# Two chained blocks on one core: up slabs on the input without its norm factor, embedding in rounded products, gate halves and residual rows in other banks

## The chip, the cores and the metric

One core of one Trainium2 chip runs the whole program. The metric is the device time of one execution in microseconds (us). The trace is that of one profiled execution; its span runs from its first to its last instruction.

## What is computed

256 tokens of width 1024 go through two blocks, one after the other, in float32. The first block has two attentions and an output projection, then a gated feed-forward layer with a short convolution over time, then a gated embedding:

```
x = x + rms_norm(mix, g_post_mix)
h = rms_norm(x, g_pre_ffn)
u = causal_depthwise_conv(h @ w_up, conv_w, conv_b)      # 1024 -> 2 x 2816, three taps
gate, val = split(u)
x = x + rms_norm((gelu(gate) * val) @ w_down, g_post_ffn)
e = p @ w_ple                                            # 256 -> 1024
g = sigmoid(rms_norm(x, g_ple_gate) @ w_ple_gate + b)
x = x + rms_norm(g * e, g_post_ple)
```

The second block modulates its norms by a condition (`mod = silu(c) @ mod_w + mod_b`), has a convolution, a sparse attention and a pooling mixer, and ends in a mixture of 32 experts (1024 -> 512 -> 1024, two experts for each token, their residual added), whose 96 weight slots of 2 MB each are all read. A last rms_norm gives the output.

## The kernel before

Each engine has a program of its own, written out by hand: `tensor` (PE), `scalar` (ACT), `vector` (DVE), `gpsimd` (POOL) and `sync` (SP). They meet only in semaphores: `wait_ge(name[key])` waits for the instruction that was issued with `then_inc(name, key)`. Each engine works strictly in its written order, so a wait holds everything behind it. SP issues all DMAs in the order of the list `STREAM`, into a ring of seven slots of 2 MB; before each it waits until the slot's last content was used (`BEFORE`, `used`). One late `used` holds all loads behind it.

A weight product is made of three "rounded" products. ACT writes the rounded weight (`hi`), DVE or POOL the rest (`lo` = weight - `hi`), the input has the same two parts, and PE multiplies `hi*hi`, `hi*lo` and `lo*hi`. There are four places for weight pairs (`weight_place`), so ACT can round at most four tiles ahead of PE. `POOL_UP` lists the rests that POOL makes. Other products are plain float32 and take PE two instructions each.

The stages that matter here, in order:

- **Output projection (`wo`)**, and after it `to_features("mix")`: PE turns the tokens back to features, DVE adds them to the residual `xT` in eight steps (`add_turned`). ACT squares `xT` (`x_squares`), PE sums the squares over features (`token_sums`), ACT copies, PE makes columns (`token_columns`), ACT takes the root and DVE its reciprocal (`joint_row`), and PE spreads the factor over all partitions (`turned_over`).
- **Up, 11 slabs (`wup`)**: only then does DVE multiply `xT` by gain and factor into `yT` (`h`), ACT round it, DVE make its rest, tile by tile. A slab j is 8 tiles k, each with 4 column blocks x 3 products of 128x256, that is 96 products in two PSUM banks. While slab j runs, `conv_step(j-1, step)` makes convolution, gelu and product of slab j-1: ACT the base tap, DVE two more taps for each of the two banks, ACT gelu, POOL the product and a rest.
- **Down (`wdown`)**: 44 weight tiles, in each 6 products of 128x512. DVE also makes 16 sums (`mod_column`) for the second block, each with a weight slot (`modw`) that SP can replace only when its fourth sum is made.
- **Embedding and gate**: `embed` has four products groups of two float32 products, in banks 5 and 6, between the turns of the tokens; `gate` has three rounded products per tile, with its halves in the banks `ZB`.
- **Second block**, up to `route`: PE adds `wout2`, DVE adds to `xT`, ACT squares, POOL and DVE add the squares, PE sums them (`cols`). `token_major` turns `xT` into rows by four times four transposes (banks `TOKB`), ACT scales them (`h`), and `over_tokens` brings the same rows into the banks `YB` once more, by products with the identity, in which the experts' sums are then accumulated: two of the four before the routing's products, two behind the first eight expert slots of group 0.
- **Experts**: 8 groups of 12 slots. After the first slots, slots 12, 13 and 14 are loaded in halves of 1 MB, each into the half of the ring that a used slot of group 0 left.

## Time and profile before

| | us |
|---|---|
| median of 3 runs | 919.2 (918.31 to 919.8) |
| profiled execution, its own time | 917.52 |
| its span | 915.6 |
| PE busy / DVE busy / ACT busy / POOL busy in the span | 769.0 / 383.0 / 328.8 / 128.0 |
| data read and written | 298.48 MB |

Busy shares are means over stages of different kinds. The chain of waits (the work that ended last, followed back) tells which engine or transfer set the end at each time, and the table of stretches what the others did meanwhile.

### The profile page before, as it was taken

To read this page: it belongs to the slowest core of one execution; us is meant where nothing else is said; L and a number is where in the kernel's file an instruction comes from. 1 tells how busy PE (TensorE), PEld (TensorE's weight loads), DVE (VectorE), ACT (ScalarE), POOL (GpSimd) and SP (SyncE) were. 2 spreads that over 40 slices of the span, in tenths; PEclk is the share of its full clock that TensorE was granted. 3 is DMA by queue.
4 is the path that set the end of the run, shared out by engine and by line. 5 is a ranking of instruction groups with operands and counts; after the bars stand their busy time and mean duration, and the time that the engine had idled before them with its cause. 6 is when DMAs were issued, how large, how long until landed. Compare 5 with 4: busy or idle time off the path is not lost.

```text
span 915.6 us, 12692 instructions
## 1 busy us (share of the span) xinstructions
PE 769.0 (84%) x5298; PEld 527.4 (58%) x5298; DVE 383.0 (42%) x838; ACT 328.8 (36%) x656; POOL 128.0 (14%) x130
## 2 busy tenths in 40 slices
PE   9999999999999999999999985668675575655575
PEld 7986579999998867898785431223221222212223
DVE  5757776667779764899613110010100100101002
ACT  5756767666665467824723010001000000000012
POOL 0021042555541033103010000000000000000000
PEclk9999999999999999999999997878778887887877
DMA  9956709755069782646579999999999999999995
GB/s 356 422 193 230 318 1 374 292 185 184 2 278 394 280 337 78 263 175 229 220 306 356 428 447 420 431 434 432 437 433 422 432 437 425 436 432 428 432 421 241
DMA packets 19359, 298.48 MB, mean 326 GB/s; under 512 B 2144, under 2 KB 2528, under 8 KB 5856
## 3 DMA queue, kind: packets, MB, share of 16 engines
q1 hardware_dynamic: 19296, 297.61, 78.7%
q8 instruction: 43, 0.70, 0.3%
q14 instruction: 20, 0.16, 0.1%
HBM read 296.55 MB, written 1.05 MB: 325 GB/s over the span
## 4 chain that ended last, share of the span: by engine, by line
PE 56%; DMA 30%; DVE 9%; ACT 3%; issue 1%; SPq 0%; DVEq 0%; ACTq 0%
PE ps L114 56%; DMA ring<-in_exps 30%; DVE ar L140 3%; DVE fr L132 2%; ACT L120 1%; DVE ar L132 1%; DVE hT L140 0%; ACT sq L120 0%; PE ps L117 0%; ACT ar L123 0%; DVE xg L140 0%; ACT ar L120 0%; ACT yT L120 0%; DVE yT L140 0%; ACT hT L120 0%
## 5 line engine op out<-in xcount | busy, mean ns | idle before, releaser
L114 PE MATMUL ps<-fr 128*128 128x256 f32 (+2 forms) x1308 | 206.7, 314 | 1.1 <-ACT fr L120 0.4
L114 PEld LDWEIGHTS ps<-fr 128*128 128x128 f32 (+1 forms) x1308 | 182.9, 189 | 19.3 <-issue 2.1
L114 PE MATMUL ps<-ring,sq 128*32 128x512 f32 x944 | 129.7, 703 | 74.9 <-DMA ring<-in_exps 74.5
L114 PE MATMUL ps<-ring,ar 128*32 128x512 f32 (+4 forms) x792 | 97.1, 594 | 49.4 <-DMA ring<-in_exps 45.4
L114 PEld LDWEIGHTS ps<-ring,sq 128*32 128x32 f32 x944 | 31.8, 126 | 163.6 <-DMA ring<-in_exps 87.9
L132 DVE TENSOR_TENSOR fr<-ring,fr 128x512 fp32r<-128x512 f32 (+1 forms) x120 | 93.8, 808 | 40.2 <-ACT fr L123 40.1
L132 DVE TENSOR_TENSOR ar<-ar,ps 128x512 f32<-128x512 f32 x9 | 6.2, 687 | 242.3 <-PE ps L114 241.3
L114 PEld LDWEIGHTS ps<-ring,ar 128*32 128x32 f32 (+1 forms) x792 | 29.8, 125 | 101.5 <-issue 50.9
L123 ACT ACTIVATE fr<-ring 128x512 fp32r<-128x512 f32 (+1 forms) x139 | 80.1, 622 | 22.6 <-PE ps L114 20.0
L123 ACT ACTIVATE ar<-ps 128x512 f32<-128x512 f32 (+4 forms) x48 | 27.2, 571 | 153.6 <-PE ps L117 130.7
L132 DVE TENSOR_TENSOR ar<-ps,ar 128x512 f32<-128x512 f32 (+6 forms) x38 | 23.4, 632 | 120.5 <-PE ps L114 120.2
L114 PE MATMUL ps<-ar 128*128 128x512 f32 (+10 forms) x328 | 65.6, 418 | 8.0 <-DVE ar L132 6.9
L120 ACT ACTIVATE sq<-ps,misc 128x128 f32<-128x128 f32 x31 | 11.9, 456 | 166.3 <-PE ps L114 166.3
L114 PE MATMUL ps<-fr,fr_h 128*128 128x256 f32 x552 | 69.7, 282 | 0.0
L114 PEld LDWEIGHTS ps<-fr,fr_h 128*128 128x128 f32 x552 | 67.7, 191 | 0.0
L114 PEld LDWEIGHTS ps<-ar 128*128 128x128 f32 (+4 forms) x328 | 36.8, 172 | 39.1 <-issue 18.8
L132 POOL TENSOR_TENSOR ar<-ar 128x128 f32<-128x128 f32 (+2 forms) x21 | 11.2, 533 | 312.5 <-DVE ar L132 311.4
L123 ACT ACTIVATE fr_h<-ring 128x512 fp32r<-128x512 f32 x66 | 40.2, 630 | 17.7 <-PE ps L114 17.6
L120 ACT ACTIVATE ar<-ps 128x768 f32<-128x768 f32 (+1 forms) x21 | 14.8, 715 | 83.3 <-PE ps L114 81.9
L114 PEld LDWEIGHTS ps<-ar,yT 128*128 128x128 f32 x256 | 30.4, 192 | 11.8 <-issue 11.5
L140 DVE SCALAR_TENSOR_TENSOR yT<-ps,cols,yT 128x255 f32<-128x255 f32 (+1 forms) x88 | 37.2, 472 | 0.0
L132 DVE TENSOR_TENSOR fr_h<-ring,fr_h 128x512 fp32r<-128x512 f32 x43 | 31.3, 730 | 13.6 <-ACT fr_h L123 13.5
(193 smaller groups left out, 896.5 us busy)
## 6 DMA issues: line engine op xcount, KB each, us to landing
ring<-in_exps SPq DMA_DIRECT2D x21, 4096.0 KB, 28.4
ring<-in_exps SPq DMA_DIRECT2D x10, 6144.0 KB, 26.9
ring<-in_modw SPq DMA_DIRECT2D x12, 2048.0 KB, 13.8
ring<-in_exps SPq DMA_DIRECT2D x12, 2048.0 KB, 12.6
ring<-in_wup SPq DMA_DIRECT2D x11, 2048.0 KB, 14.0
ring<-in_wdown SPq DMA_DIRECT2D x5, 2048.0 KB, 12.7
ring<-in_exps SPq DMA_DIRECT2D x9, 1024.0 KB, 10.8
ring<-in_win SPq DMA_DIRECT2D x4, 2048.0 KB, 11.2
```

What stands on the lines that cost most here:

```text
L114: return Issue(self.e and self.e.matmul(o, l, r, start=start, stop=stop, skip_group_check=True))
L120: return Issue(self.e and self.e.activation(o, i, f, **kw))
L123: return Issue(self.e and self.e.activation(o, i, ACT.Copy, scale=scale))
L132: return Issue(self.e and self.e.tensor_tensor(o, a, b, op))
L140: return Issue(self.e and self.e.scalar_tensor_tensor(out=o, in0=a, scalar=s, in1=b, op0=op0, op1=op1))
```

## The change

It has seven parts.

1. **Up input without the factor.** `x_hi` is now the rounded `xT * g_pre_ffn`, its rest `x_lo` follows from `xT` directly; the factor's row is made while PE works on slabs 0 and 1 and is multiplied into each slab's two result banks (`normed`, 22 DVE instructions in place in PSUM) before the convolution.
2. **Orders around it.** ACT, DVE and POOL have another order in slabs 0 and 1 and in `conv_step` (steps 3, 4, 5, 8, 9); squares are added in pairs by POOL, so that PE has four column sums in place of eight; PE makes them behind slab 0, the columns behind tile (1,0), the row behind tile (1,1). The banks of the slabs are swapped (`FB`). `mod_column` in slabs 7 to 10 stands at k = 7 in place of k = 1.
3. **Second modulation third earlier.** `mod_sum(1)` and `mod_total(1)` move from the stretch before slab 0 into the output projection.
4. **`crow`** has a place of its own and is loaded earlier, its silu moves to slab 4.
5. **Embedding** in three rounded products each; ACT and POOL make the parts of `p` and `w_ple` in the down stage.
6. **Gate halves** in other banks (`ZB`), so that the first half no longer waits for the last embedding copy; in the second block's start half a `modw` slot is worked off in quarters (`mod_quarter`).
7. **Route.** `token_major` brings the rows once, by products, straight into `YB`, where ACT reads them; `over_tokens` goes. Squares are summed by PE in two steps without DVE's addition. The halves of slots 12 to 14 take other places: half 0 of slot 12 goes to `xT`, as soon as the rows are turned, each other half one place earlier.

```
-POOL_UP = {("lo", 0, k) for k in (0, 1, 2, 3, 5, 7)} | ...
+POOL_UP = {("lo", 0, k) for k in range(6)} | ...
-        FB = (0, 1, 4, 5)
+        FB = (4, 5, 0, 1)
-        ZB = {(0, 0): 6, (1, 0): 7, (0, 1): 0, (1, 1): 1}
+        ZB = {(0, 0): 0, (1, 0): 7, (0, 1): 6, (1, 1): 1}
+        def half_place(j, h):
+            if (j, h) == (12, 0):
+                return xT
+            i, o = {(12, 1): (0, 0), (13, 0): (0, 2048), (13, 1): (4, 0), (14, 0): (4, 2048), (14, 1): (1, 0)}[j, h]
+            return slot("exps", i)[:, o:o + 2048]
...
 PE, output projection
             column_sums(5, [(tile(sq, k), act_wo["osq", k // 2]) for k in range(4)]).then_inc(pe_wo, "sums", 1)
+            mod_total(1)
 PE, before and in slab 0
-            idle_products(1, 5)
-            token_sums("mix", 2, dve_joint["mix", "mt", 1, 0])
-            idle_products(1, 5)
-            token_columns("mix", 2)
-            idle_products(2, 5)
-            pe.wait_ge(dve_joint["mix", "rrecip"])
-            turned_over(3, misc[:, 118:120]).then_inc(pe_joint, "mix", "over")
-            mod_total(1, act_wo["root", 1])
...
+                    if (j, k) == (0, 7):
+                        column_sums(2, [(tile(sq, i), pool_up["squares", i // 4]) for i in (0, 1, 4, 5)])...
+                    if (j, k) == (1, 0):
+                        token_columns("mix", 2)
+                    if (j, k) == (1, 1):
+                        pe.wait_ge(dve_joint["mix", "rrecip"])
+                        turned_over(3, misc[:, 118:120]).then_inc(pe_joint, "mix", "over")
 PE, embedding
+                pe.wait_ge(pool_gate["p_lo"], *free)
                 for k in range(2):
-                    t = pe.matmul(bank(5 + j), ar[:, ...], slot("wple", 0)[:, ...], k == 0, k == 1)
+                    pe.matmul(bank(5 + j), ph[:, c], wh, k == 0, False)
+                    pe.matmul(bank(5 + j), ph[:, c], wl, False, False)
+                    t = pe.matmul(bank(5 + j), pl[:, c], wh, False, k == 1)
-            pe.wait_ge(act_gate["e", 1, 1], dve_joint["ffn", "mt", 1, 1])
+            pe.wait_ge(dve_joint["ffn", "x", 1], dve_joint["ffn", "mt", 1, 1])
 PE, route
+                    t = pe.matmul(bank(YB[i], 128 * c, 128 * c + 128), xT[:, ...], ident, c == 0, False)
+            token_major(0)
+            pe.wait_ge(pool_out2["squares", 6])
+            square_columns(sums, True)
+            tile_logits(7)
+            pe.wait_ge(act_out2["xsq", 7])
+            square_columns(tile(sq, 3), False).then_inc(pe_route, "cols")
+            for i in (2, 1, 3):
+                token_major(i)
 ACT, before and in slab 0
+            def up_input(k):
+                act.wait_ge(dve_joint["mix", "x", k])
+                act.copy(tile(fr, k, XH), tile(xT, k), col("g_pre_ffn", k)).then_inc(act_up, "x_hi", k)
+            for i in range(4):
+                up_input(2 * i)
+                if i == 3:
+                    up_rounded(0, 6)
+                up_input(2 * i + 1)
+                if i == 3:
+                    up_rounded(0, 7)
+                act.activation(sq[:, i * 512:(i + 1) * 512], xT[:, ...], ACT.Square)...
+                if i in (1, 2):
+                    up_rounded(0, 3 + i)
+            up_rounded(1, 0)
+            up_rounded(1, 1)
+            act.wait_ge(pe_joint["mix", "sums"])
+            act.copy(sd[:, 0, :], half(2, 0)).then_inc(act_joint, "mix", "sums")
+            up_rounded(1, 2)
+            act.wait_ge(pe_joint["mix", "cols"])
+            row_root(misc[:, 116:118], ps[:, 2, S:S + 2], 32 * 1024).then_inc(act_joint, "mix", "rroot")
+            act.activation(misc[:, 2:3], eps, ACT.Gelu_apprx_tanh).then_inc(act_up, "tables")
 DVE
+            def normed(j, p):
+                u = by(bank(up_bank(j, p)), S)
+                dve.wait_ge(pe_up[j, 7], dve_joint["mix", "row"])
+                dve.tensor_tensor(u, u, wide(rb[:, 1, :], 2), ALU.mult).then_inc(dve_up, "normed", j, p)
+            for j in range(1, 11):
+                for k in range(8):
+                    if (j, k) != (1, 4):
+                        up_rest(j, k)
+                    if (j, k) == (1, 2):
+                        joint_row("mix", 116)
+                        dve.wait_ge(pe_joint["mix", "over"])
+                        dve.tensor_copy(rb[:, 1, :], half(3, 0)).then_inc(dve_joint, "mix", "row")
+                    if k == 2:
+                        normed(j - 1, 0)
+                        if j == 1:
+                            up_rest(1, 4)
+                        normed(j - 1, 1)
+                    conv_step(j - 1, k - (j == 1))
+                    if j > 6 and k == 7:
                         mod_column(j - 7)
 SP
+                        if (j, h) == (12, 0):
+                            sp.wait_ge(pe_route["tokens", 3], act_out2["xsq", 7])
+                        else:
+                            sp.wait_ge(*used("exps", *{(12, 1): (0, 0), (13, 0): (0, 1), ...}[j, h]))
+                    if j == 21:
+                        sp.wait_ge(*used("exps", 14))
```

## Rows read from the trace of the kernel before

**Rows 1.** Page, part 2: what the DMA engines moved in 40 slices

```profile
GB/s 356 422 193 230 318 1 374 292 185 184 2 278 394 280 337 78 263 175 229 220 306 356 428 447 420 431 434 432 437 433 422 432 437 425 436 432 428 432 421 241
```

**Rows 2.** Chain that ended last: start us, us, what

```profile
133.07 3.24 DVE xg L140 x8
...
146.92 216.19 PE ps L114 x1444
...
372.66 1.60 PE ps L114 x12
...
531.26 18.26 DMA ring<-in_exps
```

**Rows 3.** Stretches in the up stage: us, busy us of each engine, clock, DMA

```profile
153.00:164.50 11.50, 11.50 (x98) 11.50 (x97) 7.57 (x14) 8.64 (x15) 5.82 (x4) 1.00 1.01 428
164.50:176.00 11.50, 11.50 (x98) 11.50 (x98) 8.00 (x15) 7.36 (x14) 5.80 (x4) 1.00 0.59 241
...
222.00:233.50 11.50, 11.50 (x99) 11.50 (x98) 9.12 (x17) 7.37 (x14) 5.80 (x4) 1.00 0.52 185
```

**Rows 4.** Timeline from the residual to slab 0: start us, us, instruction

```profile
139.15 0.67 DVE L129 COPY ar<-ps 128x512 f32<-128x512 f32 x1
...
140.83 3.11 PE L114 MATMUL ps<-fr 128*128 128x256 f32 x24 [0.30 <-ACT fr L123]
...
141.45 0.42 DVE L132 TENSOR_TENSOR fr<-yT,fr 128x256 fp32r<-128x256 f32 x1
141.57 0.42 ACT L123 ACTIVATE fr<-yT 128x256 fp32r<-128x256 f32 x1 [0.49 <-DVE yT L140]
...
146.81 1.29 POOL L132 TENSOR_TENSOR fr<-ring,fr 128x512 fp32r<-128x512 f32 x1 [11.98 <-ACT fr L123]
...
147.73 1.28 ACT L120 ACT_TABLE_LOAD   x1
```

**Rows 5.** Timeline, PE's sums of four tiles and its turn of a modulation third

```profile
112.61 0.64 PE L114 MATMUL ps<-sq,con 128*32 128x256 f32 x8
...
139.87 0.66 PE L117 MATMUL ps<-con,ar 128*128 128x128 f32 x4 [0.15 <-DVE ar L129]
```

**Rows 6.** Timeline in slab 3: taps, rests alone and beside POOL, roundings

```profile
180.37 0.87 DVE L140 SCALAR_TENSOR_TENSOR yT<-ps,cols,yT 128x255 f32<-128x255 f32 x2
182.54 0.68 DVE L132 TENSOR_TENSOR fr_h<-ring,fr_h 128x512 fp32r<-128x512 f32 x1
184.94 1.14 ACT L123 ACTIVATE fr<-ring 128x512 fp32r<-128x512 f32 x2
185.59 2.41 DVE L132 TENSOR_TENSOR fr<-ring,fr 128x512 fp32r<-128x512 f32 x2 [2.37 <-ACT fr L123]
185.82 1.62 POOL L132 TENSOR_TENSOR fr<-yT,fr 128x512 fp32r<-128x512 f32 x1
```

**Rows 7.** Timeline, PE in down and in the first embedding

```profile
322.34 2.88 PE L114 MATMUL ps<-fr 128*128 128x512 f32 x12
...
327.78 1.88 PE L114 MATMUL ps<-ring,ar 128*128 128x512 f32 x4
```

**Rows 8.** Timeline, PE in the route and behind group 0's first eight slots

```profile
482.60 0.61 PE L114 MATMUL ps<-con,ar 128*128 128x1 f32 x4 [0.34 <-DVE ar L132]
...
484.41 1.95 PE L114 MATMUL ps<-con,xg 128*128 128x128 f32 x16
...
489.80 1.07 PE L114 MATMUL ps<-ring,sq 128*32 128x512 f32 x8 [0.33 <-ACT sq L120]
...
507.35 2.05 PE L114 MATMUL ps<-con,xg 128*128 128x128 f32 x16
```

**Rows 9.** Timeline, SP's issue of half 0 of slot 12

```profile
490.92 0.33 SPq L166 DMA_DIRECT2D ring<-in_exps  x1
```

**Rows 10.** Stretches around it, columns as in rows 3

```profile
489.00:500.00 11.00, 10.67 (x93) 5.02 (x96) 3.46 (x15) 2.16 (x4) 1.72 (x4) 1.00 0.78 275
500.00:520.00 20.00, 18.92 (x174) 8.25 (x166) 1.61 (x3) 2.77 (x5) 0.00 (x0) 1.00 1.01 427
```

More of the change, by code:

```diff
@@ L521, in mod_half, with mod_quarter @@
                 mod_slot(j, *free, parts=(kk,))
+            def mod_quarter(j, kk, h):
+                k, c = 2 * (j % 4) + kk, slice(256 * h, 256 * h + 256)
+                for q in range(4):
+                    t = pe.matmul(ps[32 * q:32 * q + 32, 4, c], ar[:, cond + 32 * k:cond + 32 * k + 32],
+                                  slot("modw", j)[:, 2048 * kk + 512 * q + 256 * h:2048 * kk + 512 * q + 256 * h + 256], False, True)
+                if h:
+                    t.then_inc(pe_mod, "slot", j)
             def mod_slot(j, *free, parts=(0, 1)):
@@ L1188, in tensor @@
                             first_gather(1)
-                if g == 0:
-                    for i in range(2):
-                        over_tokens(i)
                 if g == 0:
@@ L1487, in scalar @@
             up_rounded(0, 3)
-            x_squares("mix")
-            joint_row("mix", 2, 116)
-            for k in range(8):
-                act.wait_ge(dve_up["h", k])
-                act.copy(tile(fr, k, XH), tile(yT, k)).then_inc(act_up, "x_hi", k)
+            def up_input(k):
[8 more added lines that the diff above has]
+                    up_rounded(0, 7)
+                act.activation(sq[:, i * 512:(i + 1) * 512], xT[:, i * 512:(i + 1) * 512], ACT.Square).then_inc(act_joint, "mix", "xsq", i)
+                if i in (1, 2):
[8 more added lines that the diff above has]
+            act.activation(misc[:, 2:3], eps, ACT.Gelu_apprx_tanh).then_inc(act_up, "tables")
             def conv_base(j, p):
-                act.wait_ge(pe_up[j, 7], pool_up["f_lo", j - 2] if j > 1 else dve_up["x_lo", 7])
+                act.wait_ge(dve_up["normed", j, p], pool_up["f_lo", j - 2] if j > 1 else None)
                 for i in range(2):
@@ L1947, in vector @@
             mod_total(0)
-            for k in range(4):
+            out_rest(1, 0)
+            mod_sum(1)
+            for k in range(1, 4):
                 out_rest(1, k)
             out_rest(0, 4)
+            mod_total(1)
             group_factor(1)
@@ L2060, in vector @@
                     mod_column(4 + DOWN_COLUMNS.index(i))
-                if i > 3 and i % 2 == 0:
-                    conv_step(10, i // 2)
+                if i == 4:
+                    normed(10, 0)
+                    normed(10, 1)
+                if i > 5 and i % 2 == 0:
+                    conv_step(10, i // 2 - 1)
             tokens_leave("ffn", DB, pool_up["f_lo", 10])
@@ L2221, in vector @@
                 dve.scalar_tensor_tensor(tile(xT, k), bank(b, o, o + S), mod[:, 16 + k:17 + k], tile(xT, k), ALU.mult, ALU.add).then_inc(dve_out2, "x", k)
-            dve.wait_ge(pool_out2["squares", 6], act_out2["xsq", 7])
-            dve.tensor_tensor(sums, sums, tile(sq, 3), ALU.add).then_inc(dve_out2, "squares")
+            dve.wait_ge(pool_conv["pm"], pool_conv["rwg"])
+            dve.memset(few, 3.0e38).then_inc(dve_route, "few")
             dve.wait_ge(act_route["root"])
@@ L2395, in conv_step @@
                 return t
-            for j in range(11):
+            for k in range(6):
+                t = rest(pool_up, ("lo", 0, k), slot("wup", 0)[:, 512 * k:512 * k + 512], *weight_place(k), t, act_up["hi", 0, k])
+            for i in range(2):
+                pool.wait_ge(t, act_joint["mix", "xsq", 2 * i + 1])
+                o = 1024 * i
+                t = pool.tensor_tensor(sq[:, o:o + 512], sq[:, o:o + 512], sq[:, o + 512:o + 1024], ALU.add).then_inc(pool_up, "squares", i)
+            for j in range(1, 11):
                 for k in range(8):
@@ L2401, in gpsimd @@
                                  act_up["hi", j, k])
-                    if j:
-                        t = conv_step(j - 1, k, t)
-            for step in (6, 7):
+                    if j > 1 and k == 0:
+                        t = conv_step(j - 2, 9, t)
+                t = conv_step(j - 1, 8, t)
+            t = conv_step(9, 9, t)
+            for step in (8, 9):
                 t = conv_step(10, step, t)
+            p, hi, lo = p_parts()
+            t = rest(pool_gate, ("p_part",), p, hi, lo, t, act_gate["p"])
+            for q in range(4):
+                t = rest(pool_gate, ("ple", q) if q < 3 else ("p_lo",), *ple_parts(q), t, act_gate["ple", q])
             t = spread_cond(1, t, pe_down[21, 1, 1])
@@ L2538, in sync @@
                 if (name, j) == ("wup", 2):
-                    sp.wait_ge(pe_joint["mix", "sums"])
-                    sp.dma_start(sq[:, 0:1024], A["crow"]).then_inc(landed["crow"], "all")
+                    sp.wait_ge(pe_stick["values", 3])
+                    sp.dma_start(crow, A["crow"]).then_inc(landed["crow"], "all")
                 if (name, j) == ("exps", 5):
```

191 lines of the change are left out of this document (99 added, 92 removed).

## The prediction

> **What bounds the kernel now.** I read the DMA line of the page first. From the 23rd slice on (a slice is 22.9 us) the engines move 420 to 447 GB/s without a break until the last one, before that anything from 1 to 422 [rows 1]. So the experts' part is bound by the transfers, and nothing that an engine saves in there counts. The chain of waits says the same: from 531.26 on, its long pieces are expert loads [rows 2]. It also says what sets the time at which that stream begins: chains of engines, and one piece of 216.19 us in which PE alone sets the end, all of up, down and gate [rows 2]. Therefore a microsecond off that front part moves the whole stream forward by one, and beside it counts only a hole in the stream itself.
>
> In the front part the reader is to see two things. First, between the residual's eight additions (133.07) and the moment from which PE never waits (146.92) [rows 2] there is a chain of small steps: squares, sums, root, reciprocal, row, then eight rounds of `h`, `x_hi`, `x_lo`. PE's first slab product is at 140.83 [rows 4]. Second, in the slabs PE is busy 11.50 of 11.50 us with 98 products in sight, a slab of 96 therefore takes 11.5 us and a tile 1.44, while DVE has 8.00 us of work and 9.12 where a `mod_column` is added, ACT 7.4 and POOL 5.8 [rows 3]. DVE is the next bound there, with 3.5 and 2.4 us to spare.
>
> **The change part by part.**
>
> *Modulation third moved (part 3): +0.7.* PE's four transposes take 0.66 us [rows 5]. Before, they and DVE's 0.67 us copy [rows 4] lay in the wait before slab 0 and cost nothing on PE's side; now the transposes stand in the output projection, between products on which the end of that stage depends. DVE's copy hides behind PE's sums there (0.64, [rows 5]). Below nothing is excluded, and 1.4 is the other end if the copy is not hidden.
>
> *Slab 0 starts without the factor: -6.8.* `x_hi(0)` now needs only the first addition. That begins at 133.07 and takes 0.4 (3.24 for eight, [rows 2]); ACT's copy takes 0.42 [rows 4]; with two hops PE starts at about 134.05 in place of 140.83. The four weight pairs of tiles 0 to 3 are there or nearly so, as before. Is slab 0 then fed? DVE needs 8 x (0.40 + 0.42) = 6.6 us for additions and rests plus two weight rests of 0.68 [rows 6], and ends near 142.4, when PE, at 1.44 per tile, wants tile 6 at 142.7 and tile 7 at 144.1. ACT has eight inputs, four squares (0.6 each) and four roundings (0.57 each, [rows 6]), 8 us, and rounds tile 7 at about 141. The cover is thin: 0.3 us at tile 6. I put the stall at 0.1; before, four tiles took 6.09 us (140.83 to 146.92) against 5.76, so 0.3 of stall goes: net -0.2. By the rests that run beside POOL (two in 2.41 us, against 0.68 alone, [rows 6]) it could be 1.5.
>
> *The sums between the products: +1.3.* Four column sums in place of eight 0.55 (eight instructions in 0.64, [rows 5]), the columns 0.45 (four in 0.61, [rows 8]), the row 0.3. Before, all of it lay in front of slab 0, hence inside the 6.8.
>
> *Slab 1 catches up: +1.6.* Count from the end of slab 0. PE: sums to 0.55, tile 0 to 2.0, columns to 2.45, tile 1 to 3.9, row to 4.2, tile 2 to 5.6. ACT: copy of the sums to 1.05, rounding of tile 2 to 1.65, root at 2.75, then a table load of 1.28 (as that in [rows 4]) to 4.05, rounding of tile 3 to 4.65; POOL's rest of it takes 1.29 [rows 4] and is there at 5.95: PE waits 0.35. DVE: copy of the row to 4.65, first `normed` to 5.35, rest (1,4) to 6.1, or 6.7 beside POOL, second `normed` to 7.4, two taps of 0.87 [rows 6] to 9.15, then the rest of tile 5 to 9.85. PE wants it at 8.85: it waits 1.0, and 0.2 for tile 6. What is queued behind DVE's wait for the row is just this: rests, and behind them PE. The ends are 0 and 3.
>
> *Slabs 2 to 10: +0.5.* Two `normed` per slab, in place in PSUM on 128x512. No row shows that. The nearest, PSUM to SBUF on 128x512, took 0.67 [rows 4]; from below it is that, from above a rest slowed by POOL, 1.4. At 0.69 DVE goes from 8.0 to 9.4 us per slab, from 9.12 to 10.5 in slabs 7 to 10, against 11.5: PE remains the bound, but the rest of tile 6 comes 0.2 to 0.3 us before its time, as taps, POOL's product and rests fall together. I allow 0.5 in all; with 1.4 each, DVE has 10.8 and 11.9, and four slabs lose 0.4 each, others some tenths: 3 in all. The row shows that two rests of 0.68 took 2.41 us while POOL worked for 1.62 [rows 6]. The Trainium skill (SBUF — State Buffer, Who interferes with whom) gives the reason: a DVE instruction with two SBUF inputs waits for a GpSimd instruction that reads SBUF, one with at most one SBUF input does not. By that rule `normed`, with one input in PSUM, would never be held and the sum stays as it is; if it were held as the rests are, 2.5 us would be lost here.
>
> *`mod_column` at k = 7, `crow` early: 0.* The fourth column ends some 2.5 us before down begins, where it had ended about 9 us before; SP's load of `wdown` 1 and all behind it wait for that. A 2 MB slot takes 4.9 us at 430 GB/s [rows 1], with latency some 9, so it is there 6 us into down, and its first tile is wanted at 10.9 (8 tiles of 1.36). This cover, and a similar one for `wple`, whose rounding stands in ACT's row among down's, is 1.5 to 3 us; if it is gone the cost is that of the delay, 1 to 2 us.
>
> *Embedding: -1.4.* One `embed` is four instructions in 1.88 us, 0.43 apart; six rounded products are half of twelve in 2.88, so 1.4, or 1.36 at their pace [rows 7]. It saves 0.34, four times. All four lie in PE's row in front of the gate, and the new `ZB` lets the gate start when PE is free. The parts are made under down's products (ACT 5 x 0.57, POOL 5 x 1.3). 0.7 if ACT's copies hold PE.
>
> *Quarter slots: -0.4.* Between ACT's copy and the row stands a piece of 1.60 us on PE, twelve instructions [rows 2]; half of the eight modulation ones move into ACT's copy time, the other half lies behind root and reciprocal.
>
> *Route: -3.0.* PE's way to the first slot is about level: the row products (sixteen in 1.95, [rows 8]) put `cols` 0.55 later, DVE's chain loses an addition and two small steps, and the first slot no longer waits for ACT's tile. Behind the first eight slots the 2.05 us of products [rows 8] go, so slots 8 to 11 free their places 2 us earlier. What it is worth must be read in the stream: in the 11 us from 489 on it moved 275 GB/s against 427 behind [rows 10], that is 11 x (1 - 275/427) = 3.9 us of hole, since half 0 of slot 12 is issued only at 490.92 [rows 9]. Now that 1 MB (2.45 us) is issued at about 484.7, while slot 11 still flows, and each later half comes one place earlier. I expect 3.0; the ends are 2.4 (the one half) and 3.9.
>
> Sum: 0.7 - 6.8 - 0.2 + 1.3 + 1.6 + 0.5 - 1.4 - 0.4 - 3.0 = **-7.7 us**. The profiled execution has a span of 915.6 and a time of 917.52; the new one should show 907.9 and 909.8. The runs' median is 1.7 above that profiled execution, so I predict 919.2 - 7.7 = **911.5 us**.
>
> **The rivals.**
>
> *DVE becomes the bound of the slabs* (chance 0.14): `normed` at 1.4, the stretch of slab 1 at 3: 911.5 + 2.5 + 1.4 = 915.4 at the worst, 914.5 as its middle. For it speaks that DVE's margin in slabs 7 to 10 falls to 1.0; against it, PE's record of 11.50 in 11.50 with four pairs of lead.
>
> *The hole in the stream stays* (0.08): the half is there earlier, but later loads run dry, for instance the double load from slot 21 on, which now waits for slot 14 as well (some 1.8 us of PE). Then 914.5. Against it: the transfers issued by then reach some 3 us past it.
>
> *Everything is covered* (0.12): slab 1 has no stall, the hole closes wholly: 911.5 - 1.6 - 0.5 - 0.9 = 908.5.
>
> *Slower than before* (0.05): `normed` in PSUM is far slower than a read. DVE has 11.5 - 9.4 = 2.1 us left per slab, 1.0 in the last four; to eat 7.7 us over ten slabs the pair would have to take about 2.5 us more than the 1.4 that I take, each 1.9 in place of 0.69. At 2.5 each the time would be about 923. No row shows DVE writing PSUM, so I can't exclude it.
>
> *No change* (0.03): up's start is taken back by the stalls behind it and the hole is filled by later waits: 919.
>
> **How the numbers follow.** My forecast has 0.58, its own range is 909.5 to 913.5 (0.9 for the route's ends, about 1 for slab 1 and up). For 8 in 10 the range takes in the covered case and DVE's: 907.5 to 915.5. The bound of no change is 0.2%, 1.8 us, about what a measurement of this kernel can tell. Faster: 0.58 + 0.14 + 0.08 + 0.12 = 0.92; same 0.03; slower 0.05.
>
> **What would show it.** PE's first product of slab 0 about 1 us behind the first addition; slab 0 to 1 with a gap of about 1 us for tile 5 of slab 1; windows of 11.5 us in slabs 2 to 10 with PE at 11.5 and DVE at 9.4 to 10.5; a `normed` of 0.69; the gate 1.4 us earlier against down's end; no stretch under 380 GB/s behind the load of slot 11 but for a short one. I would be wrong if the slabs take over 11.7 us, if a load is late in down, or if the stream has a new hole.

## The result: 0.5% slower

The changed kernel took 923.9 us (median of 5, 923.12 to 924.38) against 918.72 us (918.31 to 919.8) for the kernel before on the same chip: a ratio of 1.0053, 95% interval 1.0041 to 1.0064. I had forecast 911.5. The sign is wrong, and the time is 8.4 us above the wider of the two ranges (907.5 to 915.5). The profiled execution has a span of 921.4 us and a time of 923.12, the one before had 915.6 and 917.52.

Stretches of the up stage in the changed kernel, slab by slab (0, 1, 2, 3, 5, 8), and then slabs 7 to 10 in one; columns as in [rows 3]:

```profile
135.50:148.70 13.20, 12.35 (x102) 11.78 (x104) 12.21 (x18) 8.43 (x17) 6.10 (x5) 1.00 0.01 2
148.70:163.30 14.60, 13.45 (x112) 12.63 (x113) 11.04 (x18) 9.50 (x18) 4.70 (x3) 1.00 0.41 145
163.30:175.90 12.60, 12.00 (x98) 11.59 (x98) 11.28 (x18) 8.35 (x16) 7.07 (x5) 1.00 0.46 168
175.90:187.50 11.60, 11.60 (x98) 11.56 (x98) 10.94 (x17) 7.81 (x14) 5.71 (x5) 1.00 0.50 182
...
199.10:212.80 13.70, 12.22 (x98) 11.61 (x97) 10.86 (x18) 10.18 (x18) 6.71 (x5) 1.00 0.42 154
...
237.30:250.80 13.50, 12.38 (x99) 11.77 (x98) 13.01 (x20) 7.68 (x14) 6.13 (x5) 1.00 0.00 0
```

```profile
224.50:277.40 52.90, 48.72 (x385) 46.61 (x384) 50.92 (x72) 31.46 (x57) 23.94 (x17) 1.00 0.14 46
```

Where [rows 3] have PE busy in all 11.50 us and DVE in 8.0 or 9.12, slabs 2 and 5 take 12.6 and 13.7 us, and slabs 7 to 10 take 52.9 in place of 46: 13.2 each, with DVE busy in 50.9 of 52.9 us. The chain of waits of the changed kernel says it as well. The piece of 216.19 us in which PE alone set the end [rows 2] is broken up, and DVE's column and rests stand in it:

```profile
232.88 2.23 DVE sq L162
235.11 2.30 DVE fr L132 x2
246.27 2.23 DVE sq L162
248.51 2.29 DVE fr L132 x2
```

One account holds forecast and result together. Each part is the time between two events that both traces have (the first of the residual's additions; the load that each slab's end sets free; the loads of the small matrices, of `wout` 1 and of the last expert weights), changed kernel minus kernel before:

| part | forecast | measured |
|---|---|---|
| up to the residual's first addition (133.07, then 134.43) | +0.7 | +1.4, of which 0.96 is there from the first loads on and no part of the change |
| from there to the end of slab 0 (19.91, then 14.29) | -7.0 | -5.6 |
| slab 1 (11.53, then 14.58) | +2.9 | +3.05 |
| slabs 2 to 10 (103.59, then 114.05) | +0.5 | **+10.5** |
| end of slab 10 to the small matrices (97.85, then 96.98) | -1.4 | -0.9 |
| to `wout` 1 (8.37, then 7.95) | -0.4 | -0.4 |
| to the last load's landing (531.27, then 530.00) | -3.0 | -1.3 |
| sum | -7.7 | +6.7 |

The tail behind the last load was 0.9 shorter, so the spans differ by 5.8. One line of the seven decides. (The shorter tail goes with a higher granted clock there and is no part of the change; see what stays open.)

### The profile page after: what moved, and what is told of

Read it like the earlier page. It is cut to its first block, busy times and chain, and to the rows that moved or that the text cites. A ratio compares the mean times of both kernels' runs of the same rounds, so it can differ in the third digit from the quotient of the medians.

```text
span 921.4 us, 12711 instructions
## 1 busy us (share of the span) xinstructions
PE 761.7 (83%) x5284; PEld 527.0 (57%) x5284; DVE 419.4 (46%) x852; ACT 336.6 (37%) x664; POOL 139.9 (15%) x137
## 3 DMA queue, kind: packets, MB, share of 16 engines
HBM read 296.55 MB, written 1.05 MB: 323 GB/s over the span
## 4 chain that ended last, share of the span: by engine, by line
PE 45%; DMA 30%; DVE 16%; ACT 6%; POOL 1%; issue 1%; SPq 0%; DVEq 0%; POOLq 0%
PE ps L114 44%; DMA ring<-in_exps 30%; DVE ar L140 3%; DVE fr L132 3%; DVE yT L140 2%; DVE fr_h L132 2%; ACT yT L120 1%; DVE sq L162 1%; ACT L120 1%; ACT fr L123 1%; POOL yT L132 1%; ACT fr_h L123 1%; DVE ps L132 1%; POOL fr_h L132 1%; DVE fr L140 1%
## 5 line engine op out<-in xcount | busy, mean ns | idle before, releaser
L114 PE MATMUL ps<-fr 128*128 128x256 f32 (+2 forms) x1332 | 214.3, 317 | 6.2 <-DVE fr L132 5.4
L114 PEld LDWEIGHTS ps<-fr 128*128 128x128 f32 (+1 forms) x1332 | 187.2, 189 | 27.4 <-DVE fr L132 9.0
L114 PE MATMUL ps<-ring,ar 128*32 128x512 f32 (+4 forms) x784 | 88.2, 575 | 52.3 <-DMA ring<-in_exps 49.1
L132 DVE TENSOR_TENSOR fr<-ring,fr 128x512 fp32r<-128x512 f32 (+2 forms) x119 | 97.1, 844 | 14.8 <-ACT fr L123 14.7
L123 ACT ACTIVATE fr<-ring 128x512 fp32r<-128x512 f32 (+2 forms) x143 | 84.8, 624 | 32.2 <-PE ps L114 29.1
L114 PEld LDWEIGHTS ps<-ring,ar 128*32 128x32 f32 (+1 forms) x784 | 26.5, 121 | 100.0 <-issue 47.5
L114 PE MATMUL ps<-ar 128*128 128x512 f32 (+10 forms) x328 | 62.3, 407 | 8.0 <-DVE ar L132 6.9
L132 DVE TENSOR_TENSOR fr_h<-ring,fr_h 128x512 fp32r<-128x512 f32 x44 | 46.9, 1075 | 7.4 <-ACT fr_h L123 7.2
L132 POOL TENSOR_TENSOR fr<-ring,fr 128x512 fp32r<-128x512 f32 x24 | 34.6, 1443 | 64.5 <-ACT fr L123 63.7
L132 POOL TENSOR_TENSOR fr_h<-ring,fr_h 128x512 fp32r<-128x512 f32 x22 | 30.5, 1386 | 66.8 <-ACT fr_h L123 66.7
## 6 DMA issues: line engine op xcount, KB each, us to landing
ring<-in_exps SPq DMA_DIRECT2D x8, 1024.0 KB, 10.3
```

Source lines behind the costliest of these rows:

```text
L114: return Issue(self.e and self.e.matmul(o, l, r, start=start, stop=stop, skip_group_check=True))
L123: return Issue(self.e and self.e.activation(o, i, ACT.Copy, scale=scale))
L132: return Issue(self.e and self.e.tensor_tensor(o, a, b, op))
```

## What stands in slabs 7 to 10

GpSimd and VectorE of the changed kernel, around the border of slabs 8 and 9 (slab 9 begins at 250.8); start us, us, instruction:

```profile
244.44 1.29 POOL L132 TENSOR_TENSOR fr_h<-ring,fr_h 128x512 fp32r<-128x512 f32 x1 [5.87 <-ACT fr_h L123]
245.81 1.62 POOL L132 TENSOR_TENSOR yT<-yT 128x512 f32<-128x512 f32 x1
248.23 1.42 POOL L132 TENSOR_TENSOR fr<-yT,fr 128x512 fp32r<-128x512 f32 x1 [0.81 <-ACT fr L123]
250.26 1.69 POOL L132 TENSOR_TENSOR fr_h<-ring,fr_h 128x512 fp32r<-128x512 f32 x1 [0.61 <-ACT fr_h L123]
```

```profile
245.15 1.13 DVE L132 TENSOR_TENSOR fr_h<-ring,fr_h 128x512 fp32r<-128x512 f32 x1
246.20 2.31 DVE L162 CUSTOM_DVE_ANT_0 sq<-ring,sq 128x1024 f32<-128x1024 f32 x1
...
248.44 2.37 DVE L132 TENSOR_TENSOR fr<-ring,fr 128x512 fp32r<-128x512 f32 x2
250.73 1.78 DVE L132 TENSOR_TENSOR fr_h<-ring,fr_h 128x512 fp32r<-128x512 f32 x1
```

Lay the two fences on top of each other. The column starts at 246.20, in the middle of POOL's product, which ends at 247.43; 1.21 us (its time in the kernel before) later it is 248.64, and the column ends at 248.51. The two rests start at 248.44; POOL's rest of `f` ends at 249.65, plus 1.2 is 250.85; they end at 250.81. The next rest starts at 250.73; POOL's ends at 251.95, plus 0.6 is 252.55; it ends at 252.51. So each of these DVE operations, which found POOL at work, stood still until POOL's ended and then took its normal time: three times 1.1 us in this slab, and 0.45 for the rest of 1.13 us at 245.15. Other DVE operations are not touched. Two factors (`normed`) and a pair of taps, and the operations of POOL that lie beside the second of each pair:

```profile
202.37 1.29 DVE L132 TENSOR_TENSOR ps<-ps,rb 128x512 f32<-128x512 f32 x2
...
207.71 0.87 DVE L140 SCALAR_TENSOR_TENSOR yT<-ps,cols,yT 128x254 f32<-128x254 f32 x2
```

```profile
202.39 1.30 POOL L132 TENSOR_TENSOR fr_h<-ring,fr_h 128x512 fp32r<-128x512 f32 x1 [1.27 <-ACT fr_h L123]
...
207.78 1.30 POOL L132 TENSOR_TENSOR fr_h<-ring,fr_h 128x512 fp32r<-128x512 f32 x1 [4.09 <-ACT fr_h L123]
```

In these rows, operations with one input in PSUM run at full speed, and those with both in SBUF wait. This is the rule of the Trainium skill (SBUF — State Buffer, Who interferes with whom) that the prediction weighed for `normed` alone. What the change has moved is seen beside the kernel before, around the same place (its slab 8 ends at 245.1), first POOL and then DVE:

```profile
240.34 1.58 POOL L132 TENSOR_TENSOR yT<-yT 128x512 f32<-128x512 f32 x1 [3.27 <-DVE yT L140]
242.00 1.29 POOL L132 TENSOR_TENSOR fr_h<-ring,fr_h 128x512 fp32r<-128x512 f32 x1
243.38 1.63 POOL L132 TENSOR_TENSOR fr<-yT,fr 128x512 fp32r<-128x512 f32 x1
```

```profile
243.15 2.41 DVE L132 TENSOR_TENSOR fr<-ring,fr 128x512 fp32r<-128x512 f32 x2 [2.37 <-ACT fr L123]
245.47 1.21 DVE L162 CUSTOM_DVE_ANT_0 sq<-ring,sq 128x1024 f32<-128x1024 f32 x1
```

There POOL's product and its rest of tile 7 lay in 2.37 us in which DVE waited for ACT, and only its rest of `f` stood beside two rests of DVE. In the changed kernel DVE has no such wait left here: four operations of POOL in a row (rest of tile 7, product, rest of `f`, rest of tile 3) each stand beside a DVE operation on SBUF, and in slabs 7 to 10 the column is one of these.

My theory was therefore, in two parts: DVE bounds the slabs, and it is full because of its added work and of the holding by POOL together. The rivals: the column's place alone, the late load of `wdown` 1, the writing of PSUM, the table switch in slab 5, and the plain number of DVE's operations.

## First experiments: which part of DVE's work it is

All runs are compared with the kernel before on their own chip (918.2 to 918.9 us); against the changed kernel I compare ratios.

**1. The column back behind tile 1.**

```
-                    if j > 6 and k == 7:
+                    if j > 6 and k == 1:
                         mod_column(j - 7)
```

> The changed kernel with mod_column in slabs 7 to 10 behind tile 1 (k == 1, as in the kernel before) in place of tile 7. Theory A (the slabs are now VectorE's, and GpSimd's operations hold VectorE's): the column no longer stands beside GpSimd's product of gate and value, where it took 2.31 us, but near the rest of f; it costs 1.2 to 2.3 us. Anything from 0 to 4 us faster than the changed kernel (923.9): 921 is my guess. Theory B (the position at k = 7 alone is at fault, the other work fits): slabs 7 to 10 come back to 11.5 us each and the time falls by 7 us, to 917. Theory C (wdown 1, which lands late, is at fault): no change, 924.

Measured: 924.18 us, ratio 1.0057 (1.0043 to 1.0072); the changed kernel's is 1.0053. No change. Slabs 7 to 10:

```profile
224.20:277.90 53.70, 49.23 (x386) 46.75 (x386) 51.57 (x73) 30.78 (x57) 24.47 (x17) 1.00 0.32 123
```

The column fell beside POOL's rest of `f` now, and was held there by the same amount:

```profile
236.65 2.31 DVE L162 CUSTOM_DVE_ANT_0 sq<-ring,sq 128x1024 f32<-128x1024 f32 x1
```

Theory B, the place of the column alone, falls, and my own guess of 3 us as well. Theory C falls too, though its "no change" was right: `wdown` 1 landed at 273.61 in place of 283.20, and nothing came of it. My term "`mod_column` at k = 7: 0" was right as to the load; its cost is that of the column in either of the two places tried, both beside work of POOL.

**2. The four columns over 8 of 1024 elements.** **3. The factor on 4 of 256 tokens.** **4. No silu of c, hence no table switch.**

```
-    t = dve.products_sum(sq[:, 1024:2048], slot("modw", j)[:, o:o + 1024], sq[:, 0:1024], mod[:, i:i + 1])
+    n = 1024 if i > 3 else 8
+    t = dve.products_sum(sq[:, 1024:1024 + n], slot("modw", j)[:, o:o + n], sq[:, 0:n], mod[:, i:i + 1])
```

```
-    u = by(bank(up_bank(j, p)), S)
+    u = by(bank(up_bank(j, p)), S)[:, :, 0:4]
-    dve.tensor_tensor(u, u, wide(rb[:, 1, :], 2), ALU.mult).then_inc(dve_up, "normed", j, p)
+    dve.tensor_tensor(u, u, wide(rb[:, 1, 0:4], 2), ALU.mult).then_inc(dve_up, "normed", j, p)
```

```
-    act.activation(sq[:, 0:1024], crow, ACT.Silu).then_inc(act_mod, "crow")
+    act.copy(sq[:, 0:1024], crow).then_inc(act_mod, "crow")
-    elif (j, k) == (5, 1):
-        act.activation(misc[:, 2:3], eps, ACT.Gelu_apprx_tanh).then_inc(act_up, "again")
```

> The changed kernel, with modulation columns 0 to 3 summed over 8 of 1024 elements (so they leave out nearly all of their work). Theory A (VectorE bounds slabs 7 to 10, at 12.6 to 13.0 us busy of 13.4): 2.3 us less per slab, slabs 7 to 10 take 11.5 to 11.7 us each, 6 to 7.5 us faster than the changed kernel: 917. Theory C (the late landing of wdown 1 or the stream sets the end): under 1 us, 923.5.

> The changed kernel with the factor in PSUM multiplied into 4 of 256 tokens only (the others are left without their norm factor); waits and order stay. Theory A (VectorE bounds every slab that is longer than 11.5 us): 1.1 to 1.3 us less in each of slabs 7 to 10, and up to 1 us less in slabs 1 and 2 together, so 5 to 6 us faster than the changed kernel: 918.5. Theory D (the factor's products in PSUM disturb TensorE's writes, so that they cost more than their 1.28 us per slab): more than 8 us faster, under 916, with the steady slabs 3, 4 and 6 shorter than 11.6 as well. Theory B (the column's place alone): under 2 us.

> The changed kernel with the silu of c in slab 4 replaced by a copy of c (the modulation columns are then made from c without its silu), so that ScalarE loads no table there and none back in slab 5. Theory A: the 2.3 us by which slab 5 is longer than 11.5 (13.8) go away: 921.6. Rival: slab 5 is long for GpSimd and VectorE's order, as slabs 1 and 2 are, and the tables lie in ScalarE's idle time (8 to 10 of 11.6 us busy): no change, 924.

These three kernels leave work out (most of four columns; the factor on 252 of 256 tokens; the silu of c) and show only what that work costs. Measured: 917.70, 919.49 and 923.11 us, ratios 0.9989 (0.9978 to 1.0), 1.0002 (0.9993 to 1.0011) and 1.0045 (1.0032 to 1.0059): 5.9, 4.7 and 0.7 us less than the changed kernel by the ratios, where I had expected 6 to 7.5, 5 to 6 and 2.3. Slabs 7 to 10 without columns, then without factor:

```profile
224.00:270.50 46.50, 46.50 (x386) 46.31 (x386) 44.28 (x73) 31.22 (x57) 23.16 (x17) 1.00 0.15 53
```

```profile
222.50:273.00 50.50, 47.89 (x386) 46.43 (x385) 45.76 (x72) 31.28 (x57) 25.51 (x17) 1.00 0.15 49
```

Without the columns the four slabs are back at PE's pace. Without the factor they give 0.6 each and slabs 1, 2 and 5 0.4 to 0.8, less than the 1.05 us that DVE saves, since DVE then waits longer for ACT's base (1.02 us in place of 0.49). So DVE's time is what bounds the long slabs. Theory D, that writing PSUM costs PE something, has nothing for it: slabs 3, 4 and 6 gained 0.1 us at most. And the table switch: in its trace slab 5 takes 11.8 us, 1.9 less, and the last load lands 2.1 earlier, but the ratios differ by 0.7 us with intervals that overlap, and the span itself is only 0.2 shorter (921.2 against 921.4). The place of my 2.3 is in the trace, its worth in the whole isn't shown. With the switch left in, another order of POOL's work also brings slab 5 to 11.5 (experiment 8).

## Second experiments: amount, or place?

**7. One more rest on VectorE.** Tile 7's rest of slabs 2 to 10 goes from POOL to DVE.

```
-POOL_UP = ... | {("lo", j, k) for j in range(1, 11) for k in (3, 7)}
+POOL_UP = ... | {("lo", j, 3) for j in range(1, 11)} | {("lo", 1, 7)}
```

> The changed kernel, with GpSimd's rest of tile 7 of slabs 2 to 10 made by VectorE. GpSimd does 1.3 us less per slab and VectorE one rest of 0.65 us more. Theory A (VectorE's rests stand still while GpSimd works on SBUF, so that a rest given to GpSimd costs VectorE about its 1.3 us): 0.3 to 0.7 us less per long slab, 1 to 3 us faster than the changed kernel: 922. Rival E (VectorE has simply too many operations, whoever works beside it): 0.65 us more in each of slabs 7 to 10 and a little in the others, 2.5 to 5 us slower: 927.

Measured: 917.88 us, ratio 0.9997 (0.9988 to 1.0006), 5.1 us faster than the changed kernel with nine rests more on the engine that bounds it. Slabs 7 to 10 have 76 DVE instructions in place of 72 and less busy time of DVE, 47.3 us in place of 50.9:

```profile
222.40:272.10 49.70, 48.20 (x386) 46.58 (x385) 47.31 (x76) 30.01 (x57) 25.64 (x13) 1.00 0.15 50
```

The plain number of operations (rival E) has the wrong sign. I had the sign, not the size, since the held operation was also the column, now 1.22 us.

**8. POOL's work beside PSUM operations.** As 7, and POOL starts only behind DVE's rest of tile 2, when the factor and the taps come.

```
                     if ("lo", j, k) in POOL_UP:
+                        if k == 3:
+                            pool.wait_ge(dve_up["lo", j, 2])
                         t = rest(pool_up, ("lo", j, k), ...)
-                    if j > 1 and k == 0:
+                    if j > 1 and k == 3:
+                        t = conv_step(j - 2, 8, t)
                         t = conv_step(j - 2, 9, t)
-                t = conv_step(j - 1, 8, t)
+            t = conv_step(9, 8, t)
```

and on ACT `f_hi` of slab j - 2 behind tile 5 in place of tile 1.

> As the kernel with tile 7's rest on VectorE, and GpSimd's other three operations of a slab start only when VectorE has made the rest of tile 2, so that they stand beside VectorE's operations on PSUM (factor and taps, 4.7 us a slab, which no GpSimd operation lengthens in the trace: 0.69 and 0.86 us with and without one beside them): order rest of tile 3, product of gate and value (now that of two slabs before), rest of f. Theory A: slabs 3 to 10 take 11.5 to 11.8 us, slabs 7 to 10 together 46 to 48 in place of 52.9, 5 to 8 us faster than the changed kernel: 917. Rival E (the number of VectorE's operations): no faster than the kernel with tile 7's rest on VectorE alone. Rival H (GpSimd's rest of tile 3 comes too late for TensorE): stalls of TensorE at tile 3 with GpSimd as releaser, up to 1 us per slab, no gain.

Measured: 914.02 us, ratio 0.9963 (0.995 to 0.9977): 8.3 us faster than the changed kernel, 3.4 faster than the kernel before. A slab without and one with a column, and then slabs 7 to 10:

```profile
174.50:186.06 11.56, 11.56 (x99) 11.56 (x98) 9.32 (x17) 7.71 (x14) 4.28 (x3) 1.00 0.50 183
```

```profile
232.14:243.66 11.52, 11.52 (x98) 11.52 (x98) 10.29 (x19) 7.71 (x14) 4.30 (x3) 1.00 0.00 1
```

```profile
220.60:267.20 46.60, 46.60 (x387) 46.48 (x387) 42.37 (x75) 31.84 (x58) 20.57 (x14) 1.00 0.16 52
```

PE is busy without a break again, DVE at 9.32 and 10.29 us, and POOL's three operations take 4.3 us a slab where in experiment 7 the same three took 6.4: the holding goes both ways. Little of it is left here: DVE's two rests (6 and 7) beside POOL's rest of `f` take 1.61 us, and two rests alone 1.28. Slab 5, with its table switch, takes 11.5 as well.

**9. The same order, tile 7's rest left to POOL.**

> The changed kernel with GpSimd's operations held back to VectorE's PSUM stretch as in the 914.0 kernel, but with the rest of tile 7 left to GpSimd. Theory A (place decides): one operation of 1.3 us per slab still stands beside VectorE's rests, of which VectorE gets back the 0.65 of its own; VectorE 10.3 + 0.6 = 10.9 of 11.5 us in slabs 7 to 10, so they still fit: within 1.5 us of 914.0. Rival E (the number of VectorE's operations made the gain): it has as few as the changed kernel and so also gains: the same 914 or less. Rival I (only the removal of tile 7's rest from GpSimd made the gain): near the changed kernel, 921 or more.

Measured: 914.11 us, ratio 0.9951 (0.9938 to 0.9963), as experiment 8. Slabs 7 to 10:

```profile
220.60:266.80 46.20, 46.20 (x387) 46.16 (x386) 43.45 (x71) 31.25 (x57) 26.04 (x18) 1.00 0.17 54
```

Set against the changed kernel it differs by the order on POOL and ACT alone, and is 9.4 us faster by the ratios. DVE is busy 43.45 us with the operations for which it was busy 50.92: the 7.5 us of difference are holding that the new order avoids. Rival I falls. This one doesn't exclude rival E; experiments 7 and 8 do, 3.1 us apart with the same operations on each engine.

**11. The opposite: POOL beside rests.** Experiment 8 with one gate more, and `f_hi` behind tile 7 on ACT:

```
                     if j > 1 and k == 3:
+                        pool.wait_ge(dve_up["conv", j - 1, 1])
                         t = conv_step(j - 2, 8, t)
```

> The 914.0 kernel with two of GpSimd's three operations of a slab (product of gate and value, rest of f) gated on VectorE's last tap instead of its rest 2, so that they stand beside VectorE's rests on SBUF; ScalarE rounds f behind tile 7. The number, sizes and owners of all operations are those of the 914.0 kernel. Theory A (VectorE's operations on SBUF stand still while GpSimd's run): VectorE's 9.3 to 10.3 us per slab become 12 to 13, slabs 7 to 10 take 12.5 to 13.2 us and the others up to 12.3: 5 to 10 us slower than 914.0, about 921. Rival E (it is the number of operations alone): no change, 914.

Measured: 925.53 us, ratio 1.0075 (1.0063 to 1.0087): 10.3 us slower than experiment 8 with the same operations. The time is on theory A's side (it had 921), but the trace isn't what it foretold. DVE was to be busy 12 to 13 us a slab; in slabs 7 to 10 it is busy 41.42 of 52.70 us, 10.4 a slab, as in experiment 8:

```profile
223.00:275.70 52.70, 47.13 (x385) 46.29 (x384) 41.42 (x76) 28.48 (x55) 22.89 (x12) 1.00 0.14 47
```

Near the end of slab 9:

```profile
257.61 1.28 DVE L132 TENSOR_TENSOR fr_h<-ring,fr_h 128x512 fp32r<-128x512 f32 x2
258.81 1.22 DVE L162 CUSTOM_DVE_ANT_0 sq<-ring,sq 128x1024 f32<-128x1024 f32 x1
```

```profile
257.78 3.41 POOL L132 TENSOR_TENSOR yT<-yT 128x512 f32<-128x512 f32 x1 [4.83 <-DVE yT L140]
```

```profile
247.79 0.63 ACT L123 ACTIVATE fr<-yT 128x512 fp32r<-128x512 f32 x1 [4.10 <-POOL yT L132]
```

DVE, which came first, runs at full speed, and POOL's product waits 2.1 us: it ends at 261.19, 1.2 behind the column. What is late then is ACT's rounding of `f`, for which ACT waited 4.10 us at the same place one slab earlier, and behind it in ACT's row the weight roundings on which DVE and PE wait. So the edit was not clean: it tested a hold and a queue at once, and its 10.3 us are no measure of what a held DVE costs.

**12. The held product, with ACT waiting later.** POOL's product gated as in 11, `f_hi` on ACT and the rest of `f` on POOL behind tile 1 of the next slab.

> The 914.0 kernel with GpSimd's product of gate and value gated on VectorE's last tap, as in the 925.5 kernel, but with nobody queued behind it: ScalarE rounds f only behind tile 1 of the next slab, and GpSimd's rest of f follows there. In the 925.5 kernel the product took 3.41 us beside VectorE's rests and column while those ran at 0.64 and 1.22 us, and what waited was ScalarE's queue. Theory J (the two engines exclude each other on SBUF, and the one that comes second waits until the other's run of operations ends, so that the price is paid by whoever is queued behind the second): the product again takes 3.4 us in slabs 7 to 10, nothing waits for it, slabs 7 to 10 take 11.5 to 11.8 us, and the time is 914 to 916. Theory A in its first form (VectorE's operations always stand still for GpSimd's): VectorE loses 1.3 to 1.6 us per slab to it and the time is 917 to 921.

Measured: 921.55 us, ratio 1.0035 (1.0021 to 1.0048): theory J's 914 to 916 missed by 5.6, theory A's 917 to 921 by 0.6, and my claim that nobody is queued there was wrong.

```profile
240.83 1.28 DVE L132 TENSOR_TENSOR fr_h<-ring,fr_h 128x512 fp32r<-128x512 f32 x2
242.04 1.22 DVE L162 CUSTOM_DVE_ANT_0 sq<-ring,sq 128x1024 f32<-128x1024 f32 x1
243.18 0.08 DVE L162 DVE_READ_ACCUMULATOR2_ANT misc<- 128x1 f32 x1
243.18 2.37 DVE L132 TENSOR_TENSOR fr<-ring,fr 128x512 fp32r<-128x512 f32 x2
```

```profile
241.00 3.41 POOL L132 TENSOR_TENSOR yT<-yT 128x512 f32<-128x512 f32 x1 [4.83 <-DVE yT L140]
```

```profile
244.44 0.63 ACT L123 ACTIVATE fr<-yT 128x512 fp32r<-128x512 f32 x1 [1.82 <-POOL yT L132]
```

```profile
163.30:174.80 11.50, 11.50 (x98) 11.50 (x97) 9.55 (x17) 7.80 (x14) 4.88 (x3) 1.00 0.50 184
...
220.90:270.20 49.30, 47.80 (x385) 46.38 (x384) 47.11 (x76) 29.51 (x55) 24.28 (x13) 1.00 0.15 49
270.20:285.80 15.60, 12.90 (x50) 10.14 (x50) 10.79 (x19) 8.15 (x16) 3.98 (x3) 0.89 0.99 420
```

The first half of J stands: POOL's product waits through two rests and the column and gets in at about 243.1, when they are through; in slabs 2 to 6, without a column, slabs take 11.52. The second half fails twice. In slabs 7 to 10 the product, once in, holds DVE's next two rests (2.37 us), and ACT waits for it (1.82): 49.3 us. And at the start of down two roundings of `f` stand before the weights in ACT's row, and PE waits 2.7 us at one place there: the last line has 15.6 us for work that took 10.4 in experiment 8. Part of that is PE's clock: behind the wait the granted clock was 0.62 from 275.66 to 280.20, and twelve products took 4.60 us in place of 2.88. So of what this kernel is slower than experiment 8, 2.7 us lie in slabs 7 to 10 and 5.2 at the start of down; the larger part says nothing on the holding.

## Third: the parts outside the up stage

**5. The route part alone, 6. everything behind the last slab, each on the kernel before.** Their edits are the diff's own pieces; 5 takes the token tiles summed in place, the two square columns, the half places of slots 12 to 14 and the gathers' banks, 6 in addition the embedding in rounded products, `ZB`, the gate's waits and `mod_quarter`.

> The kernel before, with the change's route part alone (token tiles summed in place, the square row in two parts, expert halves 12 to 14 in places of their own, the gathers' banks). Its exps 12 half should be issued some 4 us earlier than in the kernel before. Theory A (the route's gain is real and is hidden in the changed kernel by its up stage): 1.5 to 3 us faster than the kernel before, 916.5. Rival F (the early loads only fill the stream's hole and the stream loses them again between experts 12 and 20, as the changed kernel loses 1.1 of its gain there): within 1 us of the kernel before.

> The kernel before, with all of the change that stands behind the last up slab: embedding in rounded products with its parts made in the down stage, gate banks and waits, the modulation quarters, and the route part. The up stage and its norm rows are those of the kernel before. Theory A (all of the loss is the up stage's): 3 to 5 us faster than the kernel before, 914.5, slabs 11.5 us each, embedding and gate 1.2 to 1.4 us shorter. Rival G (the roundings in the down stage take back what the embedding gives, or the gain is lost in the stream): within 1 us of the kernel before or of the route part alone.

Measured: 916.45 us, ratio 0.9977 (0.9968 to 0.9986), and 915.22, ratio 0.9964 (0.995 to 0.9977). So the route alone gives 2.1 us and all late parts 3.3, as theory A had it. The stretch in which the stream had run at 275 GB/s [rows 10] is, in the changed kernel:

```profile
493.00:504.00 11.00, 10.41 (x87) 6.87 (x87) 5.95 (x34) 4.73 (x9) 1.74 (x4) 1.00 0.98 384
504.00:524.00 20.00, 19.48 (x175) 7.91 (x178) 1.99 (x5) 4.03 (x6) 0.00 (x0) 1.00 1.00 420
```

By the prediction's own formula the hole is 11 x (1 - 384/427) = 1.1 us in place of 3.9. That should have been worth 2.8, and at slot 16 the changed kernel had gained 2.5 of it. At the last load 1.3 were left; in the traces of experiments 5, 6 and 9, with the same route, 2.0, 1.0 and 1.8. The loads behind wait for slots that PE's products set free, and something there takes back a part, not always the same. By experiment 5's time my 3.0 was 0.9 too much.

**10. Experiment 8 with two edits at slabs 0 and 1.** ACT rounds tile 3 of slab 1 ahead of its wait for the sums, and POOL's second addition of squares waits for DVE's rests of slab 0.

```
             up_rounded(1, 2)
+            up_rounded(1, 3)
             act.wait_ge(pe_joint["mix", "cols"])
...
-                pool.wait_ge(t, act_joint["mix", "xsq", 2 * i + 1])
+                pool.wait_ge(t, act_joint["mix", "xsq", 2 * i + 1], dve_up["lo", 0, 7] if i else None)
```

> The 914.0 kernel with two more edits at slabs 0 and 1: ScalarE rounds tile 3 of slab 1 before it waits for the column sums (today it stands behind a table load and TensorE waits 0.99 us for it), and GpSimd's second addition of squares waits for VectorE's rests of slab 0 (which it held: 2.38 us for two, and TensorE waited 0.82 us). Theory A: 1.5 to 1.8 us faster than the 914.0 kernel: 912.4. Rival: the sums come later by the addition's delay (0.7 us) and the wait moves to them: 0 to 1 us.

Measured: 913.35 us, ratio 0.9942 (0.9929 to 0.9955), the lowest of all (its interval overlaps those of 8 and 9), 5 us under the kernel before. Against experiment 8 the medians differ by 0.7 and the ratios by 1.9, with intervals that overlap, so the two edits' 1.5 to 1.8 are neither confirmed nor excluded; in the trace slab 1 ends 1.3 earlier (161.75 in place of 163.02). The wait of 0.99 at slab 1 is gone, that of 0.83 at slab 0's tile 6 is not: it came from the input rests before it, held by POOL's first addition and its rests:

```profile
141.04 1.52 DVE L140 SCALAR_TENSOR_TENSOR fr<-xg,cols,fr 128x256 fp32r<-128x256 f32 x1
142.49 0.47 DVE L140 SCALAR_TENSOR_TENSOR xg<-ps,cols,xg 128x256 f32<-128x256 f32 x1
...
142.88 1.51 DVE L140 SCALAR_TENSOR_TENSOR fr<-xg,cols,fr 128x256 fp32r<-128x256 f32 x2
```

## Why the prediction was wrong

The step that failed is "Slabs 2 to 10: +0.5", with its bound of 3: it measured 10.5. The price of the work that I added was right: I had 0.69 for a `normed`, and it took 0.64 to 0.70. That experiment 8 shows DVE busy 9.32 and 10.29 us, near my 9.4 and 10.5, is in part luck: it has one rest more per slab (about 0.6), and the 8.0 and 9.12 that I started from already held 1.1 us in which POOL held DVE. What I had left out is that DVE's rests have no fixed price: the time held by POOL, which I took over as it stood, more than tripled in slab 8. I took POOL's work as 5.8 us on another engine. The row of two rests in 2.41 us [rows 6] was in front of me, and I used it to ask whether `normed` would be held; the question that decides is the other one, where POOL's moved product and rest of `f` would now stand. In the kernel before, part of POOL's work lay in DVE's idle time ([rows 6]: DVE had waited 2.37 us for ACT before those two rests). With 1.3 us more work and the new order there is none of it left. In slab 8 four operations are held, three by 1.1 us and one by 0.45, 3.7 us in place of 1.1, and 10.5 becomes 13. The rule that I cited there was right, and applied to the wrong operation.

Of this 10.5 us, slabs 7 to 10 are 6.8, slab 5 is 2.3 (1.9 of it by the table switch, through ACT's row, as experiment 4's trace alone shows) and slab 2 is 1.1. "`mod_column` at k = 7: 0" was wrong in the same way: its load was hidden, as I said, but not its time.

Point by point for the others. Slab 0 starts 1.1 us behind the first addition, as forecast, but takes 13.2 us: it gave 5.6 instead of 7.0. The 1.5 that I had named as the other end, for input rests beside POOL, is what came. (My cover of 0.3 us at tile 6 was not worked out cleanly either: 133.07 plus the 6.6 and 1.4 us of work named there is 141.0, not 142.4.) Slab 1's total was right (2.9, measured 3.05), but by luck: 0.98 was waited for tile 3, behind the table load, where I had 0.35, and 0.17 for tile 5, where I had 1.0; these 1.15 in place of my 1.6 leave 1.9 for the sums and what is around them, where I had 1.3. The embedding and gate gave 0.9 in the changed kernel and 1.3 in experiment 6 against 1.4; the quarters 0.4 as forecast; the route 2.1 by itself (experiment 5) instead of 3.0. Of my rivals, "DVE becomes the bound" named the right engine with the wrong price: I let it have 4 us at the worst, since I gave it only the slower `normed`. The slower side had a slow `normed` as its only mechanism, which didn't happen. Its 923 lies close to the measured 923.9 by chance, and is a wrong sum besides: at 2.5 us each the pair takes 3.6 more than I had, that is 1.5 over DVE's 2.1 in six slabs and 2.6 over its 1.0 in four, 20 us in all and 931.

What stays open: how much the table switch (experiment 4) and the edits at slab 1 (experiment 10) are worth, and which later loads take back a part of the route's gain; no run looks at those loads. On the first two the traces say something. From the last load's landing to the end they take between 9.1 us (the changed kernel) and 11.0 (experiment 4), 9.2 in experiment 8 and 10.1 in experiment 10. The last group of 32 products of 128x256 took 3.24 us in the kernel before and 3.30 and 3.33 in experiments 4 and 10, at granted clocks of 0.58, 0.56 and 0.57 (most of that stretch at the lower of the two levels); in the changed kernel and in experiment 8 it took 1.93, at 1.00. Nothing that was edited lies there. So up to 1.4 us of what the traces of experiments 4 and 10 had gained was lost again at the end, and the span of a single trace can't settle an effect of 1 or 2 us.

## What to carry to other kernels

When an operation is moved or added on VectorE or GpSimd, write down for both engines what stands beside what, and count an overlap of two operations that take all their inputs from SBUF as time of both; busy times per engine don't add up to a slab. GpSimd's work belongs beside VectorE's operations on PSUM: there it cost next to nothing, and holding it back until then was worth 9 us here (experiment 9). A wait that is put on a helper engine also moves what is queued behind its result on a third engine, as experiments 11 and 12 show.

## What I had not expected of the hardware

The holding has a direction: the one who comes second waits. A 128x512 operation of POOL took 1.3 us alone and 3.41 when it came during the first of three VectorE operations on SBUF in a row; in experiments 11 and 12 it was not let in between them but only at their end. The Trainium skill (SBUF — State Buffer, SBUF: two separate sides) says that whoever starts first holds the shared ports for the whole instruction. That agrees with VectorE's three holds of 1.1 us above. For POOL it was longer than one instruction: the product that started at 241.00 waited 2.2 us, through the rest of two VectorE rests and a whole column of 1.22. It isn't always so: in the changed kernel POOL's rest of 1.69 us at 250.26 came during the second of VectorE's two rests (they end at 250.81), was let in behind it, and the VectorE rest that follows at once was the one held (1.78). What decides whether POOL is let in after one operation or only after the run stays open.
